# Two chunks of a gated recurrence in one score product, one of them held mirrored, and a longer stretch of seven-product pairs in the second feed-forward block

## The reference, cut to what matters

```python
b = jnp.cumsum(lfb, axis=2)                              # log of the decay, within a chunk
diff = b[:, :, :, None, :] - b[:, :, None, :, :]
decay = jnp.exp(jnp.where(causal[None, None, :, :, None], diff, -jnp.inf))
attn = jnp.einsum('bhtk,bhtsk,bhsk->bhts', qb, decay, kb)
o = attn @ vb + jnp.einsum('bhtk,bhkv->bhtv', qb * jnp.exp(b), S)
S_new = jnp.exp(b_last[:, :, 0, :])[..., None] * S + jnp.einsum(
    'bhsk,bhsv->bhkv', kb * jnp.exp(b_last - b), vb)
```

## Time and profile before

| | us |
|---|---|
| runs, median (lowest to highest of 3) | 1120.07 (1118.75 to 1120.09) |
| the profiled execution | 1120.16 |
| its span, first to last instruction | 1118.2 |
| around the span | 1.96 |
| PE busy | 1106.8 (99%) |
| DVE busy | 626.9 (56%) |
| ACT busy | 522.2 (47%) |
| POOL busy | 437.1 (39%) |

### The profile page before, as it was taken

How to read it: one execution, slowest core, us unless ns; L and a number is a source line. 1 busy time by engine, 2 the same in 40 slices (tenths; PEclk the granted TensorE clock), 3 DMA queues, 4 the chain that set the end, 5 groups by cost and what they waited for, 6 DMA issues and landing times.

```text
span 1118.2 us, 17287 instructions
## 1 busy us (share of the span) xinstructions
PE 1106.8 (99%) x6358; PEld 971.0 (87%) x6358; DVE 626.9 (56%) x911; ACT 522.2 (47%) x725; POOL 437.1 (39%) x544
## 2 busy tenths in 40 slices
PE   9999999999999999999999999999999999999997
PEld 7889999988888888888888888888889999988886
DVE  6887777441222668888567123464787777440012
ACT  6545555542323555654466443354455555542221
POOL 0000000486665544434548883173000000485651
PEclk9999999999999999999999999999999999999999
DMA  7276775332323221222313442122187675332312
GB/s 240 76 210 188 194 197 169 114 112 96 113 94 111 77 76 57 76 76 76 113 57 133 163 157 76 39 81 102 45 226 188 178 197 169 114 113 96 112 57 76
DMA packets 48626, 135.33 MB, mean 121 GB/s; under 512 B 4672, under 2 KB 10944, under 8 KB 48448
## 3 DMA queue, kind: packets, MB, share of 16 engines
q1 hardware_dynamic: 43344, 118.38, 30.2%
q0 software_dynamic: 4032, 14.68, 7.7%
q10 hardware_dynamic: 1200, 1.57, 0.4%
HBM read 132.52 MB, written 2.10 MB: 120 GB/s over the span
## 4 chain that ended last, share of the span: by engine, by line
PE 53%; POOL 25%; issue 21%; DVE 0%; POOLq 0%; DMA 0%; ACT 0%; DVEq 0%; SPq 0%; ACTq 0%
POOL wl L438 25%; PE bank L1420 9%; PE bank L1422 9%; PE bank L1421 9%; PE bank L1522 4%; PE bank L1524 4%; PE bank L1523 4%; PE score L1523 3%; PE score L1522 3%; PE score L1524 3%; PE o_bank L1522 1%; PE o_bank L1524 1%; PE o_bank L1523 1%; PE bank L1479 1%; PE bank L1483 1%
## 5 line engine op out<-in xcount | busy, mean ns | idle before, releaser
L438 POOL TENSOR_TENSOR wl<-raw,wh 128x256 fp32r<-128x256 f32 x512 | 412.5, 839 | 326.0 <-ACT wh L472 281.8
L472 ACT ACTIVATE wh<-raw 128x1024 fp32r<-128x1024 f32 x124 | 130.1, 1054 | 162.2 <-PE bank L1422 158.1
L1420 PE MATMUL bank<-xh,wh 128*128 128x512 f32 x488 | 194.8, 399 | 0.0
L1422 PE MATMUL bank<-xh,wl 128*128 128x512 f32 x488 | 190.4, 390 | 0.0
L1421 PE MATMUL bank<-xl,wh 128*128 128x512 f32 x488 | 190.1, 390 | 0.0
L452 POOL DMA_DIRECT2D raw<-w_all x28 | 24.3, 869 | 330.1 <-DMA raw<-w_all 330.1
L1420 PE MATMUL bank<-zr,wh 128*128 128x512 f32 (+1 forms) x374 | 142.6, 381 | 0.0
L1422 PE MATMUL bank<-zr,wl 128*128 128x512 f32 (+1 forms) x374 | 141.7, 379 | 0.0
L1421 PE MATMUL bank<-zr,wh 128*128 128x512 f32 (+1 forms) x374 | 140.5, 376 | 0.0
L902 DVE SCALAR_TENSOR_TENSOR x<-bank,x 128x512 f32<-128x512 f32 (+1 forms) x31 | 21.3, 687 | 175.4 <-PE bank L1422 175.4
L1421 PEld LDWEIGHTS bank<-xl,wh 128*128 128x128 f32 x488 | 91.8, 188 | 19.9 <-issue 1.7
(11 more groups left out here) (304 smaller groups left out, 2493.8 us busy)
## 6 DMA issues: line engine op xcount, KB each, us to landing
raw<-w_all SPq DMA_DIRECT2D x200, 512.0 KB, 3.3
raw<-w_all POOLq DMA_DIRECT2D x28, 512.0 KB, 5.2
zf<-w_all SPq DMA_DIRECT2D x28, 256.0 KB, 4.5
x<-x_t SPq DMA_DIRECT2D x8, 256.0 KB, 6.2
out_t<-x SPq DMA_DIRECT2D x8, 256.0 KB, 2.4
raw<-w_all SPq DMA_DIRECT2D x6, 256.0 KB, 6.1
memf<-mem_t ACTq DMA_DIRECT2D x1, 1024.0 KB, 4.8
raw<-w_all ACTq DMA_DIRECT2D x2, 256.0 KB, 3.9
```

The source lines that it names most:

```text
L438: ins = nc.gpsimd.tensor_tensor(wl[:, slot, two], raw[:, slot, two], wh[:, slot, two].bitcast(f32), SUB)
L472: nc.scalar.activation(wh[:, slot, :], raw[:, slot, :], ACT.Copy).then_inc(hi_ready, 1)
L1420: nc.tensor.matmul(out_, a[0], b_[0], start=first, stop=False)
L1422: return nc.tensor.matmul(out_, a[1], b_[0], start=False, stop=last)
```

## The change

In the recurrence, the first chunk of each pair is held in reversed order. Queries of the mirrored chunk and of the plain one then lie in halves that complement each other, so that one product with 128 keys and 128 queries serves both chunks on a level: two products of 128x128 in place of four of 128x64. DVE keeps their valid scores in a common tile `tri`, and a further predicated copy in step Q (L1346 after) spreads `tri` over `attn`. What is mirrored by reading or writing backwards is split into two instructions: the reading of a q or f bank, the gating of q, the first product of step N. Values of chunks 0 and 2 are turned by PE, through `o_bank`, with a reversing matrix (`turn_v`), in slot 6. Masks for this are built once by DVE behind the first block's hidden layer (`make_masks`), half of them turned by PE ahead of the mixer's first group. `both` holds `kd` and `eb` interleaved, and the product of `kd` waits for both exponentials. In the feed-forward part, `PRE` and `ST` become lists: the second block has 4 pairs in whole groups and 16 by the scheme, and its preparation is written in another order, with the sum of squares ahead of the second group. PE's opening products are 10 in place of 8.

```diff
-PRE = 6
-ST = 14
-OLD = 4
+NF = 20
+PRE = [6, 4]
+ST = [NF - n for n in PRE]
+OLD = [n - 2 for n in PRE]
...
+        def keys_of(a, g):
+            at_ = XW * x_slot(a) + 256 * g + 128
+            return X[:, at_:at_ + 128]
+
+        def queries_of(a, g):
+
+            at_, m = XW * x_slot(a) + 256 * g, LEVELS[a]
+            halves = X[:, at_:at_ + 2 * (256 + m)].rearrange("p (s w) -> p s w", s=2)[:, :, 0:128]
+            return halves.rearrange("p s (n z m) -> p n s z m", z=2, m=m)[:, :, :, 0, :]
...
                 if a < len(LEVELS):
...
+                    mk = levels[:, a, :].rearrange("p (a n) -> p a n", a=1).to_broadcast([128, 2, 128])
+                    sc = score_bank[s % 2][:, 0:256].rearrange("p (g n) -> p g n", g=2)
+                    V_.copy_predicated(tri[:, :, :], mk, sc).then_inc(score_read, 1)
                 else:
...
+                    V_.copy_predicated(attn[:, :, :], mk, sc).then_inc(score_read, 1)
+                    dve.wait_ge(score_read, s + 1)
...
+                    V_.copy_predicated(attn[:, :, :].rearrange("p (g c) n -> p g c n", g=2), mk, both_ways)\
+                        .then_inc(attn_ready, 1)
...
                 if kind == "K":
...
+                    V_.tensor_tensor(eb_kd, last.to_broadcast([128, 2, 2, 128]), b_in, SUB).then_inc(diff_ready, 1)
                     take_scores(h, 4)
                     take_scores(h, 5)
-                    dve.wait_ge(exp_ready, EXPS * h + DIFFS)
-                    V_.tensor_tensor(kd[:, :], kd[:, :], fb[:, h % 2, :], MULT).then_inc(kd_ready, 1)
+                    dve.wait_ge(exp_ready, EXPS * (h + 1))
+                    V_.tensor_tensor(kd, kd, f_of(h), MULT).then_inc(kd_ready, 1)
...
+                    for c in range(2):
+                        out_ = by_chunk(onrm)[:, :, c, :]
+                        last = V_.tensor_tensor(out_ if c else mirrored(out_), by_chunk(o_bank[:, :])[:, :, c, :],
+                                                by_chunk(osq[:, :])[:, :, c, :], MULT)
...
+                        for p in range(2):
+                            dst = (q_of if kind == "q" else f_of)(c)[:, :, p, :]
+                            last = V_.scalar_tensor_tensor(out=dst if p else mirrored(dst), in0=by_chunk(src)[:, :, p, :],
...
             pe.wait_ge(consts_ready, 1)
-            for _ in range(8):
+            for _ in range(10):
...
+            def turn_v(t):
+
+                if t == 0:
+                    pe.wait_ge(group_read, G_V + TT + 4)
+                else:
+                    pe.wait_ge(v_ready, 1)
+                nc.tensor.matmul(o_bank[:, :], swap.bitcast(f32), V[:, t, :], start=True, stop=True).then_inc(v_turned, 1)
...
-                            for t in range(TT):
-                            last = nc.tensor.matmul(score_bank[s % 2][:, width * t:width * (t + 1)],
-                                                    lhs[:, 128 * t:128 * t + 128], rhs[:, t], start=True, stop=True)
+                            for g in range(2):
+                                last = nc.tensor.matmul(sc[:, 128 * g:128 * g + 128], keys_of(l, g), queries_of(l, g),
+                                                        start=True, stop=True)
...
+            pe.wait_ge(masks_in, 1)
+            nc.tensor.matmul(score_bank[0][:, :], swap, lower[:, 0:512], start=True, stop=True)
+            nc.tensor.matmul(score_bank[1][:, 0:384], swap, lower[:, 512:896], start=True, stop=True).then_inc(masks_out, 1)
```

More of the change, by code:

```diff
@@ L402, in pairs @@
             def pairs(u0, which):
-                for j in range(ST):
-                    u, p = u0 + 2 * (PRE + j), j % 2
+                for j in range(ST[which]):
+                    u, p = u0 + 2 * (PRE[which] + j), j % 2
                     if j < 2:
@@ L635, in ffn @@
-                with act.Fori(0, (ST - 2) // 2) as i:
+                    silu(0)
+                    ahead(u0 + 1)
+                    ahead(u0 + 2)
+                    silu(1)
+                    ahead(u0 + 3)
+                    ahead(u0 + 4)
+                    ahead(u0 + 5)
+                    silu(2)
+                    for i in range(4):
+                        x_split(i)
+                    silu(3)
+                    t_split(0)
+                    ahead(u0 + 6)
+                    ahead(u0 + 7)
@@ new lines, in ffn @@
+                    for o in range(1, 4):
+                        t_split(o)
+                    silu_new(4)
+                    ahead(u0 + 8)
+                    g2_split(u0 + 2 * pre + 1, 16 * (1 + ST[0] // 2 * which), u0 + 10)
+                    a22_split(0, 16 * (1 + ST[0] // 2 * which), u0 + 9)
+                    silu_new(5)
+                else:
+                    silu(0)
+                    ahead(u0 + 1)
+                    ahead(u0 + 2)
+                    for i in range(4):
+                        x_split(i)
+                    silu(1)
+                    ahead(u0 + 3)
+                    for o in range(4):
+                        t_split(o)
+                    silu_new(2)
+                    ahead(u0 + 4)
+                    g2_split(u0 + 2 * pre + 1, 16 * (1 + ST[0] // 2 * which), u0 + 6)
+                    a22_split(0, 16 * (1 + ST[0] // 2 * which), u0 + 5)
+                    silu_new(3)
@@ L1668, in step @@
                         ts = slice(128 * t, 128 * t + 128)
-                        last = nc.tensor.transpose(n_bank[:, ts], kd[:, ts], ident[:, :])
+                        last = nc.tensor.transpose(n_bank[:, ts], chunk_of(kd, t), ident[:, :])
                     last.then_inc(n_done, 1)
```

453 lines of the change are left out of this document (275 added, 178 removed).

## The result

The changed kernel takes 1123.28 us (median of 10 runs, 1122.58 to 1123.87), the kernel before 1119.92 beside it (10 runs): 1.0036 times as long, 95% interval 1.0027 to 1.0044. It is slower by 3.4 us where 0.7 less was forecast. The profiled execution has a span of 1121.7 us, 3.5 more than before's.

What follows compares the result with a forecast made beforehand. PE, busy 99%, was taken as the bound, with DVE's chain deciding in heads 1 to 3. Masks +1.6, head 0 -2.6, V +1.8, heads 1 to 3 +1.3, scheme -2.0, start -0.9: 1119.4 us, median 1119.2, range 1111.5 to 1123.2.

Steps and rivals of the forecast that it cites:

- Masks: Ahead of the mixer, PE's products of 512 and 384 columns that turn the masks add 1.6 us, hidden by nothing.
- V turned: In slot 6, PE's two products of 512 columns that turn V add 1.8 us, hidden by nothing.
- The copy into attn: In heads 1 and 2, the predicated copy adds 1.0 us each to DVE's chain, 2.0 in all.
- Level products: In the mixer, a level falls from 0.84 to 0.45 us on PE, saving 2.7 us a head over 7 levels.
- rival on level 1: Level 1's alternating queries make each of 8 products cost double, 1.8 us more, total 1120.7; chance 0.07.
- Head 0: Mixer's first head: PE sets the end, so the level saving counts less one 0.1 us wait, -2.6 us.
- Heads 1 to 3: Mixer: DVE's chain decides, 3.8 us added less 2.5 of waits filled, +1.3; PE's saving of 8 turns into waiting.
- The scheme: Second feed-forward block: two more pairs by the scheme of seven products save 2.0 us.
- The start: Two more opening products fill PE's gap and may bring full pace forward: -0.9 us taken, up to 1.7 won.
- The slower rival: In heads 1 to 3, DVE's chain meets POOL more often, up to +4.6 us; eight instructions give 1123.6; chance 0.12.
- Late preparation: Second block's preparation is 3 us late, undoing the scheme's 2.0, with PE waiting at its start: 1122; chance 0.06.
- DVE keeps up: All 28 mixer levels count, -11 us, total 1109.7, or 1114 with half of it; chance 0.23, wholly or half.

Runs made afterwards that it cites:

- e3: The changed kernel with its two new mask tables at the other end of memory, no instruction differing but in addresses: 1118.58 us, ratio 0.9994 to the kernel before.
- e2: The kernel before with an unused tile of 1152 bytes a partition ahead of the hidden tiles: 1124.54 us, ratio 1.0048.
- e6: e3 without the two PE products and two DVE copies that turn V: 1116.71 us, ratio 0.9979 to the kernel before.
- e7: e3 without the predicated copy that spreads tri over attn, one for each head: 1116.57 us, ratio 0.9977 to the kernel before.
- e4: The kernel before with the change of the second feed-forward block alone: 1117.11 us, ratio 0.9982.
- e13: The kernel before with 64 unused bytes ahead of the hidden tiles, moving them, cat and mh: 1128.06 us, one run, beside 1120.15.
- e14: The kernel before with 192 unused bytes ahead of the hidden tiles: 1121.26 us, one run, beside 1120.15.
- e15: The kernel before with 256 unused bytes ahead of the hidden tiles: 1118.33 us, one run, beside 1120.15.
- e10: e4 with 11 opening products in place of 8: 1117.23 us, ratio 0.9983 to the kernel before.
- e9: e4 with cat, feed-forward t tiles, hidden tiles' parts, sums and a22 placed by chosen starts modulo 256: 1120.80 us, ratio 1.0014 to the kernel before.

## Why the prediction was wrong

**The step that failed** is a term that the sum puts at nothing without a reason: it priced the instructions that the change adds, removes and moves, and took every other product at the 0.227 us of the earlier trace rows. Those rows are of `xh`, whose place the change leaves. Products from `zr` and `cat` were 0.2289 before, a row that was not read, and 0.2333 after. That is +4.7 us (e3 against after by the ratios; e2 shows it with no other change). Without it the change gives -0.7 us (e3, interval -1.7 to +0.2), and 0.7 less was forecast for the medians. In part that agreement is luck: the terms below missed by 1.2, 1.3, 0.8 and 0.9 us, and in the sum the misses cancel.

**Masks**, +1.6, mis-sized: 0.4. The product was priced by a plain f32 row, and `ubr` is fp32r: one instruction of 0.23 us for 512 columns.

**V turned**, +1.8: right (1.7 at its place in the trace, 1.87 by the medians of e6). **The copy into attn**, 2.0: right in kind, with a size of 1.3 (profiles) to 2.0 (medians) by e7.

**Level products.** 0.45 us a level was right on the wide levels only: 0.41 on 64 and 32, 0.57 on 16 and 8 (386.54 to 387.68 for both), 0.58 on 4 and 2, 0.65 on level 1. Two levels before lie 1.71 us apart from the group behind them, and the last takes 0.84, so a head saves 3 x 1.71 + 0.84 - (0.82 + 1.14 + 1.16 + 0.65) = 2.2 us, not 2.7. The sign of being right, 0.22 us a product on all levels, did not come: it is 0.205 to 0.33. The rival on level 1 is there at 0.24 us a head over the wide levels. But levels 16 and 8, with runs of 64 and 32 bytes, are dearer as well, which the 16-byte lines that the Trainium skill names ("SBUF — State Buffer", Door 1: The DMA port swizzle) do not explain.

**Head 0**, -2.6, mis-sized: -1.3. From the mixer's first group to the group behind step Q (354.76 to 402.85 before, 355.69 to 404.19 after) after takes 0.4 us more, with 1.7 for V in it. Of the 2.2 us that the products save, 0.9 went into two waits for DVE, 0.20 ahead of levels 16 and 8 and 0.68 behind levels 4 and 2, where the prediction left 0.1.

**Heads 1 to 3**, +1.3: +0.5 in e3, +1.4 in after with its 0.9 of clock. The chain through DVE was right in kind and place: PE waits 7.7 us there, at steps L1, K, Q and O. Which of its steps were priced too high the runs don't tell apart.

**The scheme**, -2.0: right (1.97 in the trace, e4), with no wait at its start.

**The start**, -0.9: the profile shows -1.8, the full-pace case, but e2, e13, e14 and e15 show the same with eight opening products, and e10 gained nothing in the median. Gaps of 0.77 to 0.99 us stand ahead of both paces here, so these rows don't bear out that the gap is the cause. Part 1 of "TensorE: Matmul & The Clock Gate" of the Trainium skill also says that the number of slow products at a kernel's start varies from run to run of the same kernel; with five quick and three slow starts of kernels with 8 opening products, these profiles agree. What the two opening products more gain was not shown, and e10 suggests about 0.

**The slower rival** named POOL. DVE's prices beside POOL are as before, so it was right in sign by chance.

**Late preparation** did not come, and **DVE keeps up** fell: the mixer gained nothing.

## What to carry to other kernels

A new table of a kilobyte can cost more than the change around it gains (here 4.7 us against 0.7), by moving the tiles behind it. Where PE sets the end, write down the start modulo 256 of every moving and stationary tile before and after an edit, and put small new tiles behind the big ones. Measure a new placement in the whole kernel: the small one gave the order for 512 columns, not the sizes (e13) and not the effect of mixed places (e9). Compare two traces by the starts of the same instructions, stretch by stretch; a shift that grows evenly through untouched code is no scheduling effect. And where a second engine is as busy as the first, price a saving by what that engine waits for.

## What the hardware showed that was not expected

- Where all moving tiles have one place, the time of a product depends on the difference of its two operands' starts in a partition, modulo 256 bytes: 0.2267, 0.2289, 0.2333, 0.2333 us in the kernel at 0, 64, 128, 192 for 512 columns of fp32r. The Trainium skill ("SBUF — State Buffer", Who interferes with whom) calls PE's two read ports, for the moving operand and for the weights, independent. These runs show that the pace depends on where the two operands lie to each other; whether the read ports are the reason, no run shows.
- Mixed places can undo a gain that uniform ones give: in e9, 39 of a down tile's 66 products take 0.2267 us, the others 0.2321 on average, and the sum is that of before.
- Behind a wait of PE the granted clock fell to between 0.57 and 0.79 over four us in some kernels (0.66 in after, 0.74 in e2, 0.78 and 0.79 in e3, 0.57 in e6), and not in others with the same wait (before). It cost 0.9 us in after, 1.5 in e2 and 1.0 in e6. In e3 it lay at 436 to 444 and left no trace at the end, since head 1's later wait took it up.
